# Two weight splits moved from VectorE to GpSimd, and a head's softmax scaling in two wide operations

## The reference

```python
s = jnp.einsum("bqghd,bngd->bghqn", qblk, k_cmp)            # compressed branch
...
s = s - slopes * dist; s = jnp.where(dist >= 0, s, NEG_INF)
p = jax.nn.softmax(s, axis=-1)                              # selected and window branch
...
o = (gblk[..., 0:1] * o_cmp + gblk[..., 1:2] * o_slc + gblk[..., 2:3] * o_win)
...
return out @ w_o                                            # output product
```

## Time and profile before

| | |
|---|---|
| Median of 3 runs | 961.37 us (959.64 to 964.77) |
| The profiled execution, its own time | 963.65 us |
| Its span, first to last instruction | 961.8 us |
| Mean granted TensorE clock | 0.998 of full speed |
| PE busy | 945.5 us (98%) |
| DVE busy | 711.6 us (74%) |
| ACT busy | 490.2 us (51%) |
| POOL busy | 87.0 us (9%) |

### The profile page before, as it was taken

The page is one execution under the profiler, slowest core; times in us unless marked ns, Lnnn a source line. Parts: engine busy times, 40 slices in busy tenths (PEclk is TensorE's granted clock), DMA queues, the critical chain, the costliest instruction groups (busy, mean ns, idle before and its releaser), DMA issues.

```text
span 961.8 us, 19359 instructions
## 1 busy us (share of the span) xinstructions
PE 945.5 (98%) x7852; PEld 911.6 (95%) x7852; DVE 711.6 (74%) x1135; ACT 490.2 (51%) x717; POOL 87.0 (9%) x132
## 2 busy tenths in 40 slices
PE   8999999999999999899999999999999999999998
PEld 8999999999999887599999999999998999999998
DVE  5896877777769878968777777698876767556554
ACT  6344644443347557846444443548667655433441
POOL 7000000000000042420000000020000000000000
PEclk9999999999999999999999999999999999999999
DMA  9746758686845662047586868436345347654611
GB/s 283 257 175 228 255 203 294 231 299 208 288 140 176 227 219 89 1 136 258 198 290 228 293 224 291 138 117 190 123 141 175 126 153 249 204 190 145 235 57 44
DMA packets 129835, 186.97 MB, mean 194 GB/s; under 512 B 6384, under 2 KB 100976, under 8 KB 129776
## 3 DMA queue, kind: packets, MB, share of 16 engines
q1 hardware_dynamic: 122000, 159.69, 50.1%
q0 software_dynamic: 6912, 25.17, 7.5%
q10 hardware_dynamic: 864, 1.29, 0.4%
HBM read 185.09 MB, written 1.05 MB: 194 GB/s over the span
## 4 chain that ended last, share of the span: by engine, by line
PE 89%; DVE 4%; ACT 3%; DMA 2%; issue 1%; SPq 1%; DVEq 0%; ACTq 0%
PE ps L1915 45%; PE ps L1993 19%; PE ps L1911 13%; PE ps L1913 4%; DMA g_raw<-in_a_w_in 2%; ACT g_hi L685 1%; PE ps L2123 1%; PE ps L2070 1%; PE ps L2188 1%; PE ps L2203 1%; SPq L528 0%; DVE g_lo L1192 0%; ACT opb_hi L703 0%; ACT e_odd L899 0%; PE ps L2315 0%
## 5 line engine op out<-in xcount | busy, mean ns | idle before, releaser
L1915 PE MATMUL ps<-opa_hi,g_hi 128*128 128x256 f32 x864 | 225.1, 283 | 2.0 <-ACT g_hi L685 1.2
L1915 PE MATMUL ps<-opa_lo,g_hi 128*128 128x256 f32 x864 | 216.5, 279 | 0.0
L1915 PE MATMUL ps<-opa_hi,g_lo 128*128 128x256 f32 x864 | 178.9, 280 | 0.0
L1310 DVE TENSOR_TENSOR g_lo<-g_raw,g_hi 128x2048 fp32r<-128x2048 f32 x54 | 123.8, 2292 | 69.3 <-ACT g_hi L759 69.3
L1915 PEld LDWEIGHTS ps<-opa_hi,g_hi 128*128 128x128 f32 x864 | 162.5, 188 | 5.6 <-issue 3.0
L1915 PEld LDWEIGHTS ps<-opa_lo,g_hi 128*128 128x128 f32 x864 | 159.2, 188 | 0.1
L1993 PE MATMUL ps<-hid_hi,d_hi 128*128 128x256 f32 x528 | 148.6, 281 | 0.0
L1993 PE MATMUL ps<-hid_lo,d_hi 128*128 128x256 f32 x528 | 148.4, 281 | 0.0
L1993 PE MATMUL ps<-hid_hi,d_lo 128*128 128x256 f32 x528 | 148.4, 281 | 0.0
L1192 DVE TENSOR_TENSOR g_lo<-g_raw,g_hi 128x2048 fp32r<-128x2048 f32 x54 | 123.5, 2289 | 29.6 <-ACT g_hi L685 26.9
L1915 PEld LDWEIGHTS ps<-opa_hi,g_lo 128*128 128x128 f32 x864 | 135.6, 188 | 0.0
(11 more groups left out here) (339 smaller groups left out, 1807.8 us busy)
## 6 DMA issues: line engine op xcount, KB each, us to landing
g_raw<-in_f_w_gu SPq DMA_DIRECT2D x44, 1024.0 KB, 8.9
ada_raw<-in_w_ada POOLq DMA_DIRECT2D x48, 512.0 KB, 6.4
d_raw<-in_f_w_down SPq DMA_DIRECT2D x22, 1024.0 KB, 5.1
g_raw<-in_w_in SPq DMA_DIRECT2D x14, 1024.0 KB, 8.4
g_raw<-in_w_gate SPq DMA_DIRECT2D x11, 1024.0 KB, 7.3
g_raw<-in_w_up SPq DMA_DIRECT2D x11, 1024.0 KB, 9.7
d_raw<-in_w_down SPq DMA_DIRECT2D x11, 1024.0 KB, 5.2
g_raw<-in_a_w_in SPq DMA_DIRECT2D x8, 1024.0 KB, 7.5
```

The costliest lines, as they stand in the source:

```text
L1310: dve.tensor_tensor(part_view(g_lo, g0 + r, True), raw_cols(c % 2, r % 2, True), part_view(g_hi, g0 + r, True).bitcast(F32), ALU.subtract) ...
L1915: mm = pe.matmul(pair(b)[:, a, :], wt[:, a * P:(a + 1) * P], xt, **st)
```

## The change

The low parts of `WO` and `WO + 1` leave DVE. POOL makes each of them in four quarters of 128x512, one behind each bias of the heads 8 to 15; the first quarter of a step waits until the high part is made. DVE waits for both once, ahead of the output product. In `normalize`, the inverted sums are first multiplied by the gates (four elements a row), and then two multiplications by a broadcast factor, of 128x512 and 128x256, take the place of four scalings of 128x256, 128x256, 128x128 and 128x128.

```diff
@@ POOL
+        def split_quarter(g, q):
+            ks = slice(2 * q, 2 * q + 2)
+            if q == 0:
+                pool.wait_ge(g_hi_made, g + 1)
+                pool.wait_ge(g_lo_made, g)
+            last = pool.tensor_tensor(part_view(g_lo, g, False)[:, ks], raw_step(g)[:, ks],
+                                      part_view(g_hi, g, False)[:, ks].bitcast(F32), ALU.subtract)
+            if q == 3:
+                last.then_inc(g_lo_made, 1)
...
             for h in range(NH):
                 if h >= 2:
                     pool.wait_ge(shifted, h - 1)
                 pool.tensor_scalar(bias_h[:, h % 2, :], dist[:, :], SLOPES[h], None, ALU.mult).then_inc(bias_made, 1)
+                if h >= 8:
+                    split_quarter(WO + (h - 8) // 4, h % 4)
@@ DVE, normalize
+                f = fac[:, s, i0:i0 + 4].rearrange("p (a b) -> p a b", a=TT)
                 own(dve.reciprocal(fac[:, s, i0:i0 + 4], zsum[:, s, i0:i0 + 4]))
-                for a, b, lo, w in SOFTMAX:
-                    x = e_of(h)[:, lo:lo + w]
-                    i = i0 + 2 * a + b
-                    last = dve.tensor_scalar(x, x, fac[:, s, i:i + 1], gates[:, a, 3 * h + 1 + b:3 * h + 2 + b],
-                                             ALU.mult, ALU.mult)
+                own(dve.tensor_tensor(f, f, gates[:, :, 3 * h + 1:3 * h + 3], ALU.mult))
+                for a, lo, w in ((1, 0, 256), (0, 512, 128)):
+                    x = e_of(h)[:, lo:lo + 2 * w].rearrange("p (b n) -> p b n", b=2)
+                    last = dve.tensor_tensor(x, x, f[:, a, :].unsqueeze(2).to_broadcast([P, 2, w]), ALU.mult)
@@ DVE, the rounds of the heads
-                if j == 3:
-                    split_g(WO)
                 if j == 4:
                     compressed_shift(1)
-                if j == 8:
-                    split_g(WO + 1)
+            dve.wait_ge(g_lo_made, WO + 2)
             add_product(WO, opb_hi, opb_lo, opb_hi_made, B_FILL["n3"], opb_made, "f_norm", 8)
```

## The result

The changed kernel takes 966.27 us in the median of 13 runs (964.71 to 968.77), the kernel before 961.39 us in as many on the same chip. The ratio is 1.0048, with a 95% interval of 1.0037 to 1.0058: 4.6 us slower, and 1.6 us past the upper end of the range I gave, 964.7 us. The profiled execution after takes 965.14 us with a span of 963.3 us.

What follows compares the result with a forecast made beforehand. PE held 89% of the last-ending chain; DVE set the end for 11.2 us in the heads. Moved splits, quarters and what they feed counted 0, the scaling a 0.21 us gain: 961.37 to 961.2 us, range 957.6 to 964.7.

Steps and rivals of the forecast that it cites:

- The third rival: Heads' scalings: each waits out a POOL quarter, up to 1.3 us, on three chain scalings 3.9 us, giving 965.1 us; chance 0.13.
- Its sign: Profile mark of DVE waiting for quarters: scalings of more than 0.7 us for 128x512, beside a quarter.
- The low parts of `WO` and `WO + 1`: Operations of 2.28 us each at 380.92 and 414.75, taken off DVE: gain 0, the first at most 2.28 us.
- Eight quarters on POOL: Heads 8 to 15: a quarter takes 1.3 us, two heads cost POOL 4.9 us against DVE's 7.0, so POOL keeps up.
- costs no one anything: A quarter starting under a new scaling of 0.6 us or less is held harmlessly while it stays below 2.3 us.
- What the quarters feed: Output product: both steps made by about 407 us, 15 us to spare for `WO`, first `F1` load earlier; all cost 0.
- The scaling: Heads' `normalize`: new form sums to 1.37 us as the old when POOL is quiet; gain 0.21 us beside a bias.
- The equal sums: With POOL quiet, old and new scaling both take 1.37 us, from reciprocal to next operation.
- The 0.21 us: Gain forecast for one of three chain scalings, head 9, where the old form lost this beside a POOL bias.
- The estimate from the Trainium skill: Scaling: 1.03 us for four old operations, 1.28 for three new; three chain scalings cost 0.7 us more, some 962.1 us.
- with POOL at work the two-input operation loses nothing: Scaling: DVE's operation at 380.92 kept 2.28 us over a bias, where the old scaling lost 0.21.
- in each case seen, it was POOL that waited: Argument against DVE waiting for quarters: in the trace, POOL waited for a two-input operation of DVE.

## Why the prediction was wrong

The third rival happened, "DVE waits for the quarters", to which I gave 0.13. Its price of a meeting was right, 1.1 us against 1.3. That its time, 965.1 us, came near the 966.27 measured is partly luck. It named the scalings of heads 8, 9 and 10; those that lost time on the path were of heads 9, 11 and 12 (391.29, 400.00 and 404.28), and 1.1 us more came from `c_tmp` and a small product, which it didn't count. Its sign, a 128x512 scaling of more than 0.7 us, didn't come either: that one kept its 0.69 us, and the 128x256 one behind it waited.

*The low parts of `WO` and `WO + 1`.* Right, gain 0: ACT releases `opa_lo` at 386.71 and at 421.24, and leaving the work out gains nothing.

*Eight quarters on POOL.* The size was right: 1.26 to 1.48 us against 1.3. The step that failed is the sentence that a meeting "costs no one anything" below 2.3 us. It only asked whether POOL keeps up. POOL did; the price fell on DVE. The sum had no term for an operation of DVE that waits for a quarter, and these waits took 4.4 us.

*What the quarters feed.* Right: nobody waits for `g_lo`, and SP's first load of `F1` comes at 406.58 in place of 417.10, with PE no earlier.

*The scaling.* The equal sums were right (1.34 us measured, 1.37 before). The 0.21 us were not: beside a bias the new form takes 1.67 against 1.58, since its small product waits. The estimate from the Trainium skill, page VectorE: DVE Perf Modes, sections The perf-mode tier table and The TRN2 errata, of 0.7 us more for three scalings, isn't borne out: the scaling alone costs 0.1 us of the stage.

*Where the reasoning broke.* I took "with POOL at work the two-input operation loses nothing" from a row beside a bias, an operation of POOL with one input: it had started 0.43 us earlier, and by then it keeps DVE out no more. And "in each case seen, it was POOL that waited" held for operations of DVE with two inputs alone. That DVE can wait stood in the trace that I had. The scaling of head 15, before, and its second operation, then POOL:

```profile
412.40 2.09 DVE L1546 TENSOR_SCALAR e_even<-e_even,fac,gates 128x256 f32<-128x256 f32 x4
412.73 0.96 DVE L1546 TENSOR_SCALAR e_even<-e_even,fac,gates 128x256 f32<-128x256 f32 x1
```

```profile
412.51 1.68 POOL L657 TENSOR_SCALAR_AFFINE_SELECT comb<-comb 4x256 f32<-4x256 f32 x2
```

2.09 us for 1.25, and 0.96 for 0.41 in the second operation, with POOL's operations starting under it. I read it past, because nothing waited for it there. And the meeting could be worked out: the quarter starts about 1.3 us behind the reciprocal of the scaling (the bias at 0.17 and its 1.17 us), just where the second wide operation runs (1.03 to 1.37 by my own sum).

The Trainium skill, page SBUF — State Buffer, section SBUF: two separate sides, has the rule that I did not draw on: of a VectorE operation with two SBUF inputs and a GpSimd operation that reads SBUF, the one that starts first holds the shared ports for its whole length, and the other waits. The quarters agree (1.52 us for 0.42), and so does the swapped order. For GpSimd operations with one input the runs show less than the whole length: 0.44 of 1.49 us.

## What to carry to other kernels

Before work is moved to GpSimd, look at what VectorE does at the moment when it will start, not only at whether GpSimd has the time: a two-input operation there stopped VectorE's operations with two inputs, and its scalings with one, nearly until it ended. Where both engines are released by the same event, the meeting can repeat round after round, and a few hundredths of a us (0.03 here) can settle which of them waits. Here either remedy helped: ordering the short operation first took the loss from 4.6 to 1.7 us, and holding the quarter until VectorE was past took it to 1.3. And work that lies in idle time, as the two splits did, is worth nothing wherever it goes, while its new place can cost.

## What the runs showed of the hardware that was not expected

A two-input operation of GpSimd (128x512, 1.27 us) keeps a VectorE operation out nearly to its end: 1.10 us of wait for one that starts 0.03 us behind it. A one-input operation keeps it out for a part only: 0.32 us for a bias of 128x384 that takes 1.17 us, and 0.44 us for 128x512 that takes 1.49 us; for an affine select of 4x256 that takes 1.03 us it was about 0.55 us. VectorE's scalings with one tensor input (four, 1.25 us) wait for a quarter as well, 2.46 us in all. And a fall of TensorE's clock to 0.84 in the mean over 10 us left the stage as long as it is at 1.00 (78.57 and 78.55 us), where VectorE's rows had no gap.
